# Modulation sums of a hybrid transformer trunk: pieces of 2 row blocks by 512 columns in place of 8 row blocks by 128

## What is computed

```python
c_act = silu(c)                                   # 1024
for l in range(2):
    mod = c_act @ ada_w[l] + ada_b[l]             # 1024 -> 6144: sh1, sc1, g1, sh2, sc2, g2
    h = rms_norm(x, norm_mix_g[l]) * (1 + sc1) + sh1
    y = even_mixer(h) if l == 0 else odd_mixer(h)  # conv + retention | stick-breaking attention
    x = x + g1 * y
    h = rms_norm(x, norm_ffn_g[l]) * (1 + sc2) + sh2
    x = x + g2 * (silu(h @ w_gate) * (h @ w_up)) @ w_down
```

## Time and profile before

| | us |
|---|---|
| median of 3 runs | 2928.9 (2928.38 to 2937.35) |
| the profiled execution's own time | 2935.44 |
| its span | 2932.8 |
| PE busy in it | 2658.1 (91%) |
| DVE busy in it | 1601.7 (55%) |
| POOL busy in it | 982.3 (33%) |
| mean granted TensorE clock | 0.945 |

### The profile page before, as it was taken

One profiled execution on the slowest core, in us unless ns is written; L12 is line 12 of the kernel. 1 busy time (PEld: TensorE's weight loads), 2 busy tenths in 40 slices (PEclk: granted clock), 3 DMA queues, 4 the chain that ended last, 5 costly groups with the idle time before them and its releaser, 6 DMA issues. The chain is left out here.

```text
span 2932.8 us, 36076 instructions
## 1 busy us (share of the span) xinstructions
PE 2658.1 (91%) x11394; PEld 2129.9 (73%) x11394; DVE 1601.7 (55%) x2882; ACT 475.8 (16%) x847; POOL 982.3 (33%) x1604
## 2 busy tenths in 40 slices
PE   2898989699999999999878899897799999999998
PEld 2687777577777777777666676675578888888886
DVE  5747778566444444444857777778573223332222
ACT  2000111110000000000235554554110000000001
POOL 2234223333333333334222222224053444334330
PEclk7799999899999999999889999997899999999998
DMA  6334233502222222222210000001311111111101
GB/s 215 108 107 130 86 86 93 172 15 72 72 72 75 75 72 72 72 82 82 94 33 29 30 29 30 29 29 51 125 44 43 46 55 50 50 43 50 50 29 58
DMA packets 278367, 201.90 MB, mean 69 GB/s; under 512 B 5994, under 2 KB 247812, under 8 KB 278148
## 3 DMA queue, kind: packets, MB, share of 16 engines
q1 hardware_dynamic: 262996, 159.94, 18.5%
q10 hardware_dynamic: 15280, 40.90, 3.7%
HBM read 179.84 MB, written 20.97 MB: 68 GB/s over the span
## 5 line engine op out<-in xcount | busy, mean ns | idle before, releaser
L513 PE MATMUL psG<-h_hi,w_split 128*128 128x512 f32 x2496 | 1004.2, 402 | 66.3 <-DVE h_lo L1112 34.4
L490 POOL TENSOR_SCALAR w_split<-w_raw 128x256 fp32r<-128x256 f32 x800 | 366.8, 486 | 1863.8 <-PE psG L513 655.3
L518 PE MATMUL psG<-h_lo,w_split 128*128 128x512 f32 x2496 | 987.7, 396 | 0.0
L519 PE MATMUL psG<-h_hi,w_split 128*128 128x512 f32 x2496 | 985.8, 395 | 0.0
L494 POOL TENSOR_TENSOR w_split<-w_raw,w_split 128x256 fp32r<-128x256 f32 x800 | 624.4, 813 | 0.0
L513 PEld LDWEIGHTS psG<-h_hi,w_split 128*128 128x128 f32 x2496 | 478.8, 192 | 189.8 <-issue 50.0
L519 PEld LDWEIGHTS psG<-h_hi,w_split 128*128 128x128 f32 x2496 | 477.9, 191 | 102.7
L518 PEld LDWEIGHTS psG<-h_lo,w_split 128*128 128x128 f32 x2496 | 479.2, 192 | 98.9 <-issue 3.0
L1381 DVE TENSOR_TENSOR hid<-sil,psG 128x512 f32<-128x512 f32 x88 | 60.5, 688 | 666.2 <-PE psG L519 666.1
L1391 DVE SCALAR_TENSOR_TENSOR xT<-psG,mod,xT 128x512 f32<-128x512 f32 x352 | 260.7, 748 | 174.6 <-PE psG L519 173.4
L513 PE MATMUL psG<-hid_hi,w_split 128*128 128x512 f32 x704 | 282.1, 401 | 29.0 <-DVE xT L1391 25.5
(11 more groups left out here) (142 smaller groups left out, 2217.5 us busy)
## 6 DMA issues: line engine op xcount, KB each, us to landing
ada_raw<-in_ada_w SPq DMA_DIRECT2D x80, 512.0 KB, 4.1
w_raw<-in_ffn_w_gate SPq DMA_DIRECT2D x44, 512.0 KB, 3.9
w_raw<-in_ffn_w_up SPq DMA_DIRECT2D x44, 512.0 KB, 4.0
w_raw<-in_ffn_w_down SPq DMA_DIRECT2D x44, 512.0 KB, 4.3
w_raw<-in_ev_w_in SPq DMA_DIRECT2D x28, 512.0 KB, 5.4
w_raw<-in_od_w_qkv SPq DMA_DIRECT2D x24, 512.0 KB, 3.7
ada_first<-in_ada_w SPq DMA_DIRECT2D x4, 2048.0 KB, 12.7
x_spill<-xT ACTq DMA_DIRECT2D x2, 4096.0 KB, 11.7
```

The source lines that it names most:

```text
L490: nc.gpsimd.tensor_scalar(slot[:, 0, part], raw[:, part], 1.0, 1.0, ALU.mult, ALU.mult).then_inc(hi_done, 1)
L513: mm = nc.tensor.matmul(o, st[0], mv[0], start=first, stop=False, **kw)
L518: nc.tensor.matmul(o, st[0], mv[1], start=False, stop=False, **kw)
L519: return nc.tensor.matmul(o, st[1], mv[0], start=False, stop=end, **kw)
```

## The change

A piece is now 2 row blocks by 512 columns (4 tiles): again 512 KB, but 2 instructions of 512 columns on DVE. Four pieces make a group of 4 tiles, summed in one accumulator of 512 columns. There are again 80 pieces: 4 per iteration in conv (2 iterations), 8 in ret (4), 4 in the first ten iterations of ffn0, none in its last. The misc uses of ret become six. In ret, SP's loop is unrolled and its order is slab 0, pieces 0 and 1, slab 1, pieces 2 and 3, slab 2, pieces 4 and 5, slab 3, pieces 6 and 7. The head statistic's `misc` numbers (PE's `stat`, ACT's waits) change from 2 + 2h to 3 + 2h. `mod_a` is gone.

```diff
-ADA_FREE = 3 * KT
+ADA_FREE = 4
+ADA_COLS = 4 * P
+ADA_PIECES = 4
...
-    ("conv", 2, dict(slab=6, step=12, misc=1, ada=6, group=1)),
-    ("ret", 4, dict(slab=4, step=8, misc=5, ada=6, group=1)),
+    ("conv", 2, dict(slab=6, step=12, misc=1, ada=4)),
+    ("ret", 4, dict(slab=4, step=8, misc=6, ada=8)),
...
-    ("ffn0", CHUNKS, dict(slab=6, step=24, misc=1, ada=4, group=1)),
+    ("ffn0", CHUNKS, dict(slab=6, step=24, misc=1, ada=4)),
...
-                total[kind] = total.get(kind, 0) + iters * n
+                turns = CHUNKS - 1 if name == "ffn0" and kind in ("misc", "ada") else iters
...
-        ada_raw = [at(f"ada_raw{n}", QO + (37 + 4 * n) * KB, [KT, P]) for n in range(2)]
-        ada_acc = at("ada_acc", QO + 45 * KB, [6, P])
+        ada_raw = [at(f"ada_raw{n}", QO + (37 + 4 * n) * KB, [KT // ADA_PIECES, ADA_COLS]) for n in range(2)]
+        ada_acc = at("ada_acc", QO + 45 * KB, [4, P])
...
-        ADA_AFTER = {"conv": {k: (k,) for k in range(6)},
-                     "ret": {0: (0,), 1: (1, 2), 2: (3,), 3: (4, 5)},
+        ADA_AFTER = {"conv": {0: (0,), 1: (1,), 3: (2,), 4: (3,)},
+                     "ret": {0: (0, 1), 1: (2, 3), 2: (4, 5), 3: (6, 7)},
                      "ffn0": {0: (0,), 1: (1,), 3: (2, 3)}}
...
+        def ada_cols_of(phase, i, g):
+
+            first_group, per = {"conv": (4, 1), "ret": (6, 2), "ffn0": (14, 1)}[phase]
+            return 4 * (first_group + g) + i * (4 * per)
...
-                sp.wait_ge(ada_step, ADA_FREE + KT * n - KT)
+                sp.wait_ge(ada_step, ADA_FREE + 2 * n - 2)
...
-                l, c = tiles(phase, i, k)
-                sp.dma_start(ada_raw[static % 2][:], cols(w["ada_w"][l], c * P)).then_inc(ada_in[static % 2], 16)
+                g, part = divmod(k, ADA_PIECES)
+                c = ada_cols_of(phase, i, g)
+                l = 1 if phase == "ffn0" else c // MOD if phase == "ret" else 0
+                rows = w["ada_w"][l][2 * P * part:2 * P * part + 2 * P, bass.ds((c - l * MOD) * P, ADA_COLS)]
+                sp.dma_start(ada_raw[static % 2][:], rows.rearrange("(k p) c -> p k c", p=P)).then_inc(ada_in[static % 2], 16)
...
                         sp.sem_inc(sp_turn, 1)
                         sp.dma_start(slab_ap(w_raw[static % RAW][:], phase, s), slab_src(phase, i, s)).then_inc(raw_in[static % RAW], 16)
+                        if last:
+                            continue
                         for k in ADA_AFTER.get(phase, {}).get(s, ()):
                             ada(phase, i, k)
-                loop(sp, iters, body)
+                if phase == "ret":
+                    for i in range(iters):
+                        body(i)
+                elif phase == "ffn0":
+                    loop(sp, iters - 1, body)
+                    body(iters - 1, True)
+                else:
+                    loop(sp, iters, body)
...
                 def one(g, mk):
-                    static = C.at("ada", phase, i, tiles_n * (g + 1))[1]
-                    pe.wait_ge(ada_step, ADA_FREE + KT * static)
+                    pieces = C.at("ada", phase, i, ADA_PIECES * (g + 1))[1]
+                    pe.wait_ge(ada_step, ADA_FREE + 2 * pieces)
                     misc(phase, i, mk, [lambda k=k: nc.tensor.matmul(
                         psM[:, k:k + 1], ada_acc[:, k], consts[:, 5, 0:1], start=True, stop=True)
-                        for k in range(tiles_n)])
+                        for k in range(4)])
...
                 v_turn(1)
+                ada_group("ret", i)(0, 2)
                 for t, (h, j) in enumerate(RET_TILES):
...
                     if t == 9:
-                        ada_group("ret", i)(0, 3)
+                        ada_group("ret", i)(1, 4)
...
                     for h in range(NH):
-                        if h == 1 and final(i) and next_norm:
-                            ada_group(phase, i)(0, 0)
...
-                per = C.per[phase]["ada"]
-                turns = per // 2 * 16
-                dve.wait_ge(ada_in[static % 2], (static // 2 + 1) * 16 + i * turns)
-                acc = ada_acc[:, k % (per // C.per[phase]["group"])]
-                for kt in range(KT):
-                    src, cc = ada_raw[static % 2][:, kt], c_act[:, kt:kt + 1]
+                dve.wait_ge(ada_in[static % 2], (static // 2 + 1) * 16 + i * (C.per[phase]["ada"] // 2 * 16))
+                acc = ada_acc[:].rearrange("p k c -> p (k c)")
+                for half_ in range(2):
+                    kt = 2 * (k % ADA_PIECES) + half_
+                    src, cc = ada_raw[static % 2][:, half_], c_act[:, kt:kt + 1]
                     if kt:
-                        dve.wait_ge(ada_step, ADA_FREE + KT * n + kt)
+                        dve.wait_ge(ada_step, ADA_FREE + 2 * n + half_)
                         V.scalar_tensor_tensor(acc, src, cc, acc, ALU.mult, ALU.add).then_inc(ada_step, 1)
                     else:
                         V.tensor_scalar(acc, src, cc, None, ALU.mult).then_inc(ada_step, 1)
...
-            def ada_cols(phase, i, g, mk, runs):
+            def ada_cols(phase, i, mk, c):

                 dve.wait_ge(misc_done, M(phase, i, mk))
-                for r, (p0, l, c, n) in enumerate(runs):
-                    at_ = bass.ds(l * MOD + c, n)
-                    ins = V.tensor_tensor(mod[:, at_], psM[:, p0:p0 + n], vecA[:, at_], ALU.add)
-                    ins.then_inc(misc_read if r == len(runs) - 1 else mod_a, 1)
+                at_ = bass.ds(c, 4)
+                V.tensor_tensor(mod[:, at_], psM[:, 0:4], vecA[:, at_], ALU.add).then_inc(misc_read, 1)
...
                         if h == 1:
-                            ada("conv", i, 3 * j + 2)
+                            ada("conv", i, 2 * j + 1)
...
                         if h == 0:
-                            for k in range(2):
-                                ada("conv", i, 3 * j + k)
+                            ada("conv", i, 2 * j)
...
-                ada_cols("conv", i, 0, 0, [(0, 0, 2 * KT + 4 * i, 4), (4, 1, 2 * i, 2)])
+                ada_cols("conv", i, 0, ada_cols_of("conv", i, 0))
...
             def ret(i):
-                for k in range(2):
-                    ada("ret", i, k)
+                ada("ret", i, 0)
...
                     if e < 3:
-                        ada("ret", i, e + 2)
+                        ada("ret", i, e + 1)
...
                     if t == 0:
                         v_lo(1)
-                    if t == 2:
-                        ada("ret", i, 5)
+                        ada_cols("ret", i, 2, ada_cols_of("ret", i, 0))
+                    if t in (1, 3, 5, 7):
+                        ada("ret", i, ADA_PIECES + t // 2)
                     if t == 9:
                         finish(0)
                     if t == 11:
-                        ada_cols("ret", i, 0, 3, [(0, 0, 3 * KT + 6 * i, 6)])
+                        ada_cols("ret", i, 4, ada_cols_of("ret", i, 1))
...
-                            if phase == "ffn0":
+                            if phase == "ffn0" and not final(i):
                                 ada(phase, i, e)
...
-                        if phase == "ffn0" and h == (0 if final(i) else 1):
-                            ada_cols(phase, i, 0, 0, [(0, 1, 4 + 4 * i, 4)])
-                            if final(i):
-                                gains()
+                        if phase == "ffn0" and h == 1 and not final(i):
+                            ada_cols(phase, i, 0, ada_cols_of(phase, i, 0))
+                        if phase == "ffn0" and h == 0 and final(i):
+                            gains()
...
             dve.wait_ge(misc_read, C.base["norm1"]["misc"])
-            dve.wait_ge(mod_a, 2)
```

More of the change, by code:

```diff
@@ L108, in __init__ @@
             for kind, n in per.items():
-                total[kind] = total.get(kind, 0) + iters * n
+                turns = CHUNKS - 1 if name == "ffn0" and kind in ("misc", "ada") else iters
+                total[kind] = total.get(kind, 0) + turns * n
     def at(self, kind, phase, i, k):
@@ L236, in build @@
         c_steps = sem("c_steps")
-        mod_a = sem("mod_a")
         raw_in = [sem(f"raw_in{n}") for n in range(RAW)]
@@ L398, in loop @@
                     body(i)
-        def tiles(phase, i, k):
-            if phase == "conv":
-                return (0, 2 * KT + k + i * 4) if k < 4 else (1, k - 4 + i * 2)
-            if phase == "ret":
-                return 0, 3 * KT + k + i * 6
-            return 1, 4 + k + i * 4
+        def ada_cols_of(phase, i, g):
+            first_group, per = {"conv": (4, 1), "ret": (6, 2), "ffn0": (14, 1)}[phase]
+            return 4 * (first_group + g) + i * (4 * per)
         def qkv_step(phase, e):
@@ L448, in _, with body @@
             for phase, iters, P_ in STREAM:
-                def body(i):
+                def body(i, last=False):
                     for s in range(P_):
@@ L559, in ada_group @@
             def ada_group(phase, i):
-                per = C.per[phase]
```

(17 more changed lines are left out.)

## The result

The kernel after takes 2898.53 us (median of 4 runs, 2895.74 to 2906.76), the kernel before on the same chip 2931.82 (4 runs, 2928.38 to 2937.35). The ratio is 0.9892 with a 95% interval of 0.9869 to 0.9916: faster by 1.1%. The forecast was 2895 us. The profiled execution of the kernel after took 2895.74 us, its span is 2893.9, 38.9 less than the span before.

The account below looks back on a forecast made before the run. PE bounds the kernel, and DVE matters only where PE waits for it. ffn0 -43.3, conv -5.1, ret projections +9.8 and tiles +5 sum to -33.6: 2901.8 us profiled, 2895 us median, range 2878 to 2912 us.

Parts of the forecast that it names:

- the 0.25 us left for waiting: ffn0's nine middle iterations: 0.25 us of PE waiting allowed in each, within a gain of 33.8 us.
- the cover is gone to the last tenth: ffn0 down projection: PE follows the xT update at 912.8, just when its banks run out.
- First and last iteration: ffn0: the first was to gain 4.5 us, the last, with no piece and no group, 5.0 us.
- Four times the columns cost twice the time: DVE sums: 128 columns take 407 ns and 512 take 795, about 0.28 us fixed per instruction.
- SP's order: conv: slab 3 issued behind slab 2, long before it is needed, removes PE's 4.09 us wait, plus 1.6 of clock.
- The v slab's lateness: ret projections: v slab queued behind piece 3, +1.0 us in three iterations and +4.8 in the first.
- the gate slab's: ret projections: gate slab hangs on piece 3, ready at +35.9 and wanted at +35.4, +0.5 us in each iteration.
- The pieces at tiles 1 and 3: ret tile loops: these stand beside a gate quarter and ACT's copy of the output and cost nothing.
- The relief of DVE: Rival: freeing DVE helps ret too, which gives 0 in place of +14.8, for a total of 2880 us; chance 0.17.
- contention: Rival: contention keeps the ffn0 wait alive, 0.8 us more an iteration plus clock, +21, for 2916 us; chance 0.10.
- ret's late slabs: Rival: two late-slab waits an iteration each take the clock down, 1.6 us each, +12.8, for 2912 us; chance 0.12.
- The small fixed cost: Rival: DVE's fixed cost per instruction is the skill page's small one, pieces bring 0.9 us, for 2921 us; chance 0.01.

Follow-up runs that it names:

- the added instructions: Kernel after with one or two more 512-column scalar_tensor_tensor ahead of the last piece of each ffn0 iteration: 2910.32 and 2924.62 us.
- the moved old piece: Kernel before, old pieces kept, the fourth of each ffn0 iteration moved behind the eviction of the down projection's fourth product: 2904.35 us, ratio 0.9911.
- the order put back: Kernel after with conv's third and fourth pieces again ahead of later slabs on SP's queue: 2907.24 us, conv 156.52 us.
- the late-pieces kernel: Kernel after with ret's third and fourth tile-loop pieces moved from tiles 5 and 7 to 10 and 11, their group products behind the last tile: 2899.5 us.
- the new shape with places chosen anew: Kernel after with ret's slabs ahead of pieces, late pieces, first group's products moved up and the fourth ffn0 piece moved: 2872.79 us, ratio 0.9797 to the kernel before.

## Why the prediction was right, step by step

**ffn0** was right in cause and size. The middle iterations were to give 33.8 us and gave 34.3; the 0.25 us left for waiting was 0.12 once in nine. The statement that the cover is gone to the last tenth was a little too strict: the added instructions put it at 0.4 us. First and last iteration were right within 0.3. The last piece takes 1.68 us in eight iterations and 2.03 in one, for which 2.26 at most was set. "Four times the columns cost twice the time" held at 816 ns. By the medians (352 and 281 ns for an old instruction, 752 and 480 for a new one) a piece is 1.2 us shorter; at this place it is 2.8, because beside POOL each instruction is slower and there were eight of them. The Trainium skill's fixed cost ("VectorE: DVE Perf Modes", section on the TRN2 errata), about 150 cycles, would have given the piece 1.4 us and a saving of 0.9, an estimate; both savings here are larger.

What the prediction did not see is that the shape was not needed for this gain. Its steps priced the piece and the place together, and the moved old piece tells them apart.

**conv** was right in its sum, -5.8 for -5.1, with the POOL wait gone and 2.4 us back beside norm0's tiles for 1.6. But it gave 4.1 of the 5.1 us to SP's order, and the order put back took 1.6: the shorter pieces had part in the rest.

**ret, projections.** The v slab's lateness was right: 0.92, 1.06 and 0.96 us in three iterations for 1.0; in the first, 2.5 us here and 3.6 to 4.5 in four other profiles of unchanged ret, for 4.8. The term that failed is the gate slab's, +0.5 in each of four: PE never waits for it. With the first iteration's it makes this row 4.4 us too high. SP's order as the cause was shown by turning it round.

**ret, tiles.** The sum (+4.7 for +5) is right by luck in part: it was to be +2.0 an iteration, less 3 for the clock, and came as -0.2, -0.6, +2.9 and +2.6, while profiles of the same code differ by 3.6 us. The mechanism is seen in the waits: of the `r_wp` waits, 16.5 us before and 23.7 after, those at tiles 6 to 9, which the forecast named, rose from 2.6 to 17.8 us, and those at tiles 0 to 5 fell from 10.7 to 3.0. With the pieces of tiles 5 and 7 late they are 7.6 at tiles 6 to 9 (with POOL's splits gone from the loops too). The pieces at tiles 1 and 3, which the sum took at nothing, were not free: with them out as well, 2.5 to 3.3 us of 6.5 to 7.9 are left there.

**Rivals.** The relief of DVE did not carry ret; contention did not keep the ffn0 wait in most iterations, though the rare blocked copy is a form of it that I had not listed; ret's late slabs did not take the clock down in this profile (1.00 in all four projections), but they can: in three of the four other profiles of this ret it is 0.95 in the first iteration's, behind waits of 2.16 to 2.57 us, and 0.96 behind 3.90 us in the late-pieces kernel. Behind the 0.6 to 0.8 us of the later iterations it never fell. The small fixed cost is refuted by the outcome and by the medians above. The median is 3.5 us above the forecast, while the profiled execution, 2895.74, is 6 below the 2901.8 that its own sum gave. So it is partly luck that the median came so near: the stretches gained 5.3 us more than the sum, most of it in ret's projections, and the medians gained only 33.3, because the profiled execution of the kernel before lies 3.6 above its median and that of the kernel after 2.8 below its own.

Two slips in the working changed nothing: 2 x 2.97 - 1.31 - 1.58 is 3.05 and not 2.9, and the bounds named for the range add up to 2912 at its upper end and not to 2906.

## What to carry to other kernels

Before reshaping work on an engine that is half idle, look at the place where it stands: moving one old piece by four evictions gave 33.2 us, and the new shape with places chosen anew is 60 us under the kernel before (2872.79 for 2933.14). After a wait is gone, add a known instruction at its place: the point where it begins to cost tells how much cover is left. And judge a queue's order with what it keeps apart: slabs brought forward on SP took 5.4 us off the projections, and the tile loops behind them were 8.1 longer. Where a stretch differs between two kernels, look at its granted clock first: two profiles of one program gave 157 and 170 us for the same four loops.

## What was not expected of the hardware

A VectorE copy of 128x512 from SBUF to SBUF was held for 5.5 to 14.2 us instead of 0.43 while GpSimd ran splits back to back, the longest through some 25 of its instructions, and in eleven of sixteen cases let go 0.3 us after they paused. The Trainium skill ("SBUF — State Buffer", section on who interferes with whom) has an exclusive lock on a port pair that the two engines share, held for a whole instruction, the other blocking until then. The trace agrees that the loser stands still, and goes beyond it: the copy lost to many instructions in a row. Most copies at the same place lost little (0.43 to 1.7 us).

The granted clock after a wait is not a fixed price: behind 1.87 us in ffn0 it fell to 0.50 in one iteration and held in another, and behind 2.45 us in conv it held. At ret's first v slab it held behind 2.18 us in the kernel after and fell behind 2.18 us in the kernel with the fourth ffn0 piece moved.
